# Hybrid layers and a matrix-memory block on one core: transfer order, places of the modulation chunks, and attention by pairs of heads

## What is computed

```
for l in 0, 1:                                  # two hybrid layers
    proj = x @ w_in[l]
    y = [retention(rq,rk,rv) * silu(rg),        # 4 heads of 64, rotary, decay, normalised
         nsa(nq, compressed, selected, window keys) * silu(ng),   # 8 query heads, 2 key heads
         rg_lru(conv(lx)) * silu(lg)]           # a linear recurrence over the tokens
    x = layer_norm(1.41 * x + y @ w_out[l])
# one conditioned block
sh1, sc1, g1, sh2, sc2, g2 = silu(c) @ w_ada + b_ada        # w_ada is 1024 x 6144
h_lat, h_ctx = modulate(x), modulate(ctx)       # h_ctx uses the c_ctx version of sh1, sc1
m = mlstm(h_lat, h_ctx)                         # 4 heads of 128, both directions
a = window_attention(h_lat, h_ctx, sink)        # 8 query heads, 2 key heads of 64
x = x + g1 * ((sigmoid(gm)*(m @ w_bm) + sigmoid(ga)*(a @ w_ba)) @ w_out)
x = x + g2 * peer(modulate(x))                  # 16 of 16384 experts for each token and head
```

## Time and profile before

| | |
|---|---|
| median of three executions | 1475.07 us (1467.1 to 1476.45) |
| profiled execution, device time | 1466.19 us |
| its span in the trace | 1464.3 us |
| TensorE busy | 1241.4 us (85%) |
| VectorE busy | 819.8 us (56%) |
| ScalarE busy | 283.9 us (19%) |
| GpSimd busy | 314.4 us (21%) |
| mean granted clock of TensorE | 0.927 of full |
| moved by DMA | 385.69 MB |

### The profile page before, as it was taken

How to read it: one execution, slowest core, us unless ns; L and a number is a source line. 1 busy time by engine, 2 the same in 40 slices (tenths; PEclk the granted TensorE clock), 3 DMA queues, 4 the chain that set the end, 5 groups by cost and what they waited for, 6 DMA issues and landing times.

```text
span 1464.3 us, 13967 instructions
## 1 busy us (share of the span) xinstructions
PE 1241.4 (85%) x4984; PEld 741.6 (51%) x4984; DVE 819.8 (56%) x2091; ACT 283.9 (19%) x868; POOL 314.4 (21%) x278
## 2 busy tenths in 40 slices
PE   6997799978998999998797999877877397777787
PEld 4865467845873767764356565333323143333332
DVE  0746744366522265455326667676666767767654
ACT  0113200213322112222011222111111111111111
POOL 0000000000000010000002445544444264545430
PEclk9999699988999999989798999999999699999989
DMA  7651234751222443431137899999999899999995
GB/s 302 233 230 58 115 114 160 281 224 59 115 68 105 151 149 139 172 144 58 45 128 315 296 416 420 421 421 421 420 420 420 348 421 420 421 419 422 420 421 224
DMA packets 48708, 385.69 MB, mean 263 GB/s; under 512 B 5632, under 2 KB 7424, under 8 KB 9088
## 3 DMA queue, kind: packets, MB, share of 16 engines
q0 software_dynamic: 36864, 268.45, 44.5%
q1 hardware_dynamic: 11776, 116.35, 21.1%
HBM read 383.73 MB, written 1.05 MB: 263 GB/s over the span
## 4 chain that ended last, share of the span: by engine, by line
PE 58%; DMA 27%; DVE 7%; ACT 4%; issue 2%; POOL 1%; SPq 0%; DVEq 0%; POOLq 0%; ACTq 0%
DMA arena<-peer_uv_in,arena 23%; PE bank L468 22%; PE bank L474 14%; PE bank L1003 14%; DMA wring<-w_in 2%; DMA wring<-peer_uv_in,arena 2%; PE bank L509 2%; DVE arena L1413 1%; PE bank L675 1%; DVE arena L1421 1%; DVE arena L2023 1%; PE bank L830 1%; PE bank L819 1%; ACT arena L1079 1%; PE bank L875 1%
## 5 line engine op out<-in xcount | busy, mean ns | idle before, releaser
L1003 PE MATMUL bank<-arena 128*128 128x512 f32 x480 | 231.3, 626 | 47.8 <-ACT arena L1391 24.6
L1003 PE MATMUL bank<-wring,arena 128*128 128x512 f32 x368 | 188.1, 652 | 77.8 <-ACT arena L1391 77.8
L468 PE MATMUL bank<-wring,hT 128*128 128x256 f32 (+2 forms) x672 | 211.4, 472 | 19.0 <-DMA wring<-w_in 12.6
L474 PE MATMUL bank<-hT,wring 128*128 128x256 f32 (+1 forms) x1152 | 217.7, 350 | 5.7 <-issue 2.2
L474 PEld LDWEIGHTS bank<-hT,wring 128*128 128x128 f32 x1152 | 191.5, 194 | 33.8 <-issue 10.4
L2023 DVE CUSTOM_DVE_ANT_0 arena<-arena 128x1024 f32<-128x1024 f32 x120 | 147.0, 1226 | 91.0 <-DMA arena<-peer_uv_in,arena 90.7
L1003 PEld LDWEIGHTS bank<-arena 128*128 128x128 f32 x480 | 95.0, 201 | 172.7 <-issue 141.3
L2079 POOL TENSOR_TENSOR small<-small,const 128x1 f32<-128x1 f32 (+3 forms) x18 | 16.1, 894 | 762.5 <-DVEq L1425 625.8
L468 PEld LDWEIGHTS bank<-wring,hT 128*128 128x128 f32 x672 | 129.5, 197 | 98.6 <-issue 72.4
L2103 POOL DMA_INDIRECT arena<-peer_uv_in,arena x120 | 142.3, 1186 | 142.5 <-PE bank L1003 134.7
L1003 PEld LDWEIGHTS bank<-wring,arena 128*128 128x128 f32 x368 | 71.2, 201 | 182.2 <-ACT arena L1391 106.3
(11 more groups left out here) (194 smaller groups left out, 1154.5 us busy)
## 6 DMA issues: line engine op xcount, KB each, us to landing
wring<-w_in SPq DMA_DIRECT2D x23, 2048.0 KB, 8.1
wring<-ada_in SPq DMA_DIRECT2D x12, 2048.0 KB, 8.2
wring<-wo_in SPq DMA_DIRECT2D x6, 2048.0 KB, 8.2
wring<-pq_in SPq DMA_DIRECT2D x4, 2048.0 KB, 9.0
wring<-cmp_in SPq DMA_DIRECT2D x2, 2048.0 KB, 8.8
wring<-br_in SPq DMA_DIRECT2D x2, 2048.0 KB, 10.1
wring<-w1b_in SPq DMA_DIRECT2D x2, 1120.0 KB, 8.4
const<-const_in SPq DMA_DIRECT2D x1, 2012.5 KB, 14.3
```

What stands on the lines that cost most here:

```text
L468: ins = pe.matmul(bank[:, 0:cols], lhs[k], w[:, k, 0:cols], start=(k == 0), stop=(k == n - 1))
L474: ins = pe.matmul(bank[:, at:at + n_tok], w[:, k, col:col + P], rhs[:, k, :], start=(k == 0), stop=(k == KC - 1))
L1003: ins = pe.matmul(sums_of[half][:, :], diag[:, at % NDIAG, :], v_row[slot_of[at]][:, half * 512:(half + 1) * 512], start=(n == 0), stop=(n ...
```

## The change

- **Chunk order.** Modulation chunks 0 and 1 stay in layer 0, chunks 2 and 3 go to layer 1, chunk 4 to the end of layer 1, chunks 5 to 7 into the block's projections. `w1` chunks 5 and 6 follow `cmp` directly.
- **First transfers.** x tile 0 goes first, then the identity, then the first half of `w1` chunk 1 with a semaphore of its own, its second half, x tile 1, and `w1` chunk 0 ahead of the parameters and constants. In layer 0 TensorE does `rqk` of both tiles before `lxg` of both.
- **VectorE.** `lru_scan` and `retention(0)` stand in front of the loop. No modulation in rounds 0 to 3 of either layer; chunk 4 in rounds 5 to 7 of layer 1. Chunk 5 after the last rows of `hl`, chunk 6 after the copies of `aq`, chunk 7 after the forget-gate rows.
- **Gate vectors.** `context(10..13)` leave layer 1 and stand around the projection `mq`; the first waits for `ada_bias` 2, the second for 3.
- **Attention** goes over eight rounds of two heads, one of each key group. Scores of the two use the two halves of the array's rows, values the two halves of its columns and come out transposed; probabilities are scaled before their transposes, as in the hybrid layers, so the transposes to `aT` fall away. Two branch gates stand in each of rounds 1 to 6.

The diff, cut to its core:

```diff
-            mods = [("ada", 0, n) for n in ((0, 1, 2) if layer == 0 else (3, 4, 5, 6, 7))]
+            mods = [("ada", 0, 2 * layer), ("ada", 0, 2 * layer + 1)]
             chunks += [("w1", layer, 1), ("w1", layer, 0), ("w1", layer, 2), mods[0], ("w1", layer, 3), mods[1]]
-            chunks += [("w1", layer, 4), ("cmp", layer, 0)] + mods[2:-1] + [("w1", layer, 5)]
-            chunks += [("w1", layer, 6), mods[-1]] if layer else [mods[-1], ("w1", layer, 6)]
-            if layer == DEPTH - 1:
-                chunks += [("w2c", 0, 0), ("w2c", 0, 1)]
-            chunks += [("wo", layer, 0), ("wo", layer, 1)]
-        chunks += [("w2", 0, c) for c in (4, 5, 0, 2, 1, 3)]
+            chunks += [("w1", layer, 4), ("cmp", layer, 0), ("w1", layer, 5), ("w1", layer, 6)]
+            if layer == 0:
+                chunks += [("wo", 0, 0), ("wo", 0, 1)]
+        chunks += [("w2c", 0, 0), ("w2c", 0, 1), ("wo", 1, 0), ("ada", 0, 4), ("wo", 1, 1), ("ada", 0, 5)]
+        chunks += [("w2", 0, 4), ("w2", 0, 5), ("ada", 0, 6), ("w2", 0, 0), ("w2", 0, 2), ("ada", 0, 7), ("w2", 0, 1), ("w2", 0, 3)]
...
+                x_columns(0)
+                query_rows(0)
+                if L:
+                    lru_columns(0)
+                x_columns(1)
+                query_rows(1)
+                if L == 0:
+                    lru_columns(0)
+                lru_columns(1)
...
+            def attn_scores(p):
+                t, r = rounds[p]
+                for g in range(2):
+                    half = slice(g * HD, (g + 1) * HD)
+                    bank = job(("as", 2 * p + g))
+                    finish(pe.matmul(bank[:, :], aqT[half, r, t * P:(t + 1) * P], akT[half, :], start=True, stop=True),
+                           ("as", 2 * p + g))
...
+                for s in range(4):
+                    for g in range(2):
+                        half = slice(g * HD, (g + 1) * HD)
+                        ins = pe.matmul(bank[half, r * P:(r + 1) * P], akv[:, s, P + g * HD:P + (g + 1) * HD],
+                                        softT[:, p % 2, g * 512 + s * P:g * 512 + (s + 1) * P], start=(s == 0), stop=(s == 3))
...
+            for p in range(len(rounds)):
+                attn_transposes(p)
+                if p + 2 < len(rounds):
+                    attn_scores(p + 2)
+                if p:
+                    attn_values(p - 1)
+                if 1 <= p < 7:
+                    branch_gate(2 * p - 2)
+                    branch_gate(2 * p - 1)
+            attn_values(len(rounds) - 1)
...
-                    if i == 1:
-                        for t_ in range(TT):
-                            taken(pe, ("ao", t_))
-                            transposes(("aT", t_), [a_lat[:, t_, j * P:(j + 1) * P] for j in range(4)])
...
                 nsa_scale(0)
+                lru_scan()
                 gate_rows_t(0)
                 gate_rows_t(1)
+                retention(0)
                 for p in range(len(rounds)):
...
-                    if p == 0:
-                        lru_scan()
-                    if p in (0, 1):
-                        retention(p)
-                    if p < 4:
-                        modulation(7 if L else 2, (p,))
+                    if p == 1:
+                        retention(1)
+                    if L and p >= 5:
+                        modulation(4, ((0, 1), (2,), (3,))[p - 5])
...
+            def attn_scale(p):
+                t, r = rounds[p]
+                for g in range(2):
+                    taken(dve, ("as", 2 * p + g))
+                dve.wait_ge(sem("sink_exp"), p + 1)
+                e = 2 * (p % 4)
+                link(tt(es[:, e:e + 2], es[:, e:e + 2], den[:, t, r:8:4], ALU.add))
+                link(dve.reciprocal(es[:, e:e + 2], es[:, e:e + 2]))
+                both = soft[:, p % 2, :].rearrange("p (g k) -> p g k", g=2)
+                link(tt(both, both, every(es[:, e:e + 2], 512, 2), ALU.mult), "attn_scaled")
...
+            attn_max(0)
+            attn_max(1)
+            attn_scale(0)
+            for p in range(len(rounds)):
+                bank = full(dve, ("aT_", 2 * p + 1))
+                free(dve.tensor_copy(softT[:, p % 2, 512:1024], bank[:, :]), ("aT_", 2 * p + 1))
+                if p + 1 < len(rounds):
+                    attn_scale(p + 1)
+                if p + 2 < len(rounds):
+                    attn_max(p + 2)
+                modulation(8 + p // 2, (2 * (p % 2), 2 * (p % 2) + 1))
+                if p == 4:
+                    attn_out(0)
```

More of the change, by code:

```diff
@@ L1567, in _ @@
                 free(ins, ("kcvc", L))
-                modulation(1 if L == 0 else 4)
+                modulation(2 * L + 1)
+                if L:
+                    add_bias(0, 2)
+                    gain(1, V_GMIX, "mix_gain")
                 if L == DEPTH - 1:
```

209 lines of the change are left out of this document (98 added, 111 removed).

## The result

| | before | after |
|---|---|---|
| median of the runs, us | 1474.54 (1467.1 to 1476.45, 4 runs) | 1434.99 (1433.3 to 1438.13, 4 runs) |
| profiled execution, us (span) | 1466.2 (1464.3) | 1433.3 (1431.5) |
| mean granted clock of TensorE | 0.927 | 0.93 |

The ratio is 0.9743, 95% interval 0.9705 to 0.9781: 2.6% faster, 1435 as forecast. The profiled executions stand 32.9 us apart and the medians 39.6, where the sum said 35.6: the profiled execution of the kernel before is one of its fast ones, 1466.2 where most lie near 1475. Nearly the right total hides terms that missed by up to 7 us in both directions, and most of what follows is about those.

The account below looks back on a forecast made before the run. It took TensorE, then DMA in the gathers, as successive bounds. Terms 5.0 + 13.5 + 11.3 + 6.0 - 1.9 + 0.6 + 1.1 = 35.6 us gave 1430.6 (profile) or 1439.5 (median); forecast 1435, range 1420 to 1460.

Parts of the forecast that it names:

- The frame: Whole kernel: the final gather stage is DMA-bound and untouched, so each microsecond won ahead of it comes out at the end.
- Start: First transfers: half chunk lands near 7.7 us, `rqk` starts near 8, `w1` chunk 0 is released 5.0 us earlier.
- Layer 0's loop: Modulation passes and scan leave VectorE's path, shortening TensorE's waits: 13.5 us won, bounds 10 and 16.
- the walk: Round-by-round reckoning with VectorE's durations; layer 0: round 2 at 140.4, round 3 at 147.6, round 4 at 153, round 6 at 168.
- `w1` chunk 5: Layer 1: its earlier load removes a wait of 8.27 us and 3.0 us of half clock in `rvg`: 11.3 us won.
- Layer 1's loop: Four modulation passes go and the scan moves: 6.0 us won, between 7.1 and 4.7 depending on the clock.
- Projections: End of layer 1 and the block's projections: weights queued behind modulation chunks and moved contexts cost 1.9 us, bounds +2 and -9.
- rival (2): Weight chunks queued behind VectorE's modulation each cost 8.3 + 3.0 us; with four caught the kernel ends at 1480; chance 0.05.
- Attention: Pairing heads gains 3.6 us and loses 3.0 to a low clock in the opening gap: 0.6 won, bounds -4 and +4.
- Rival (4): The clock holds through the new gaps and attention's pairs gain their 8 us: 1424 us; chance 0.12.
- Rival (3): Attention becomes bound by VectorE, exposing 2.3 us in each of six rounds, 14 us: 1449 us; chance 0.08.
- The stage behind attention: ScalarE no longer copies `aT` ahead of the exponents VectorE waits for: 1.1 us won, bounds 0 and 1.5.

Follow-up runs that it names:

- after_again: The changed kernel, unedited, run and profiled once more as the control: 1433.82 us, ratio 0.9727 to the kernel before.
- quarters: The changed kernel with the first half chunk of `w1` chunk 1 loaded as two transfers of 0.5 MB: 1434.09 us, ratio 0.9713.
- b_order: The kernel before with layer 1's `w1` chunk 5 loaded one place earlier, the eight modulation passes left where they were: 1478.95 us, ratio 1.0018.
- b_scan_in_front: The kernel before with only the scan and retention(0) moved in front of the loop, in both layers: 1466.9 us, ratio 0.9936.
- a_warm: The changed kernel with unneeded matmuls filling TensorE's waits ahead of rounds 1, 3 and 4 of layer 0's loop: 1435.01 us, ratio 0.9728.
- the gateless round: Round 2 in the changed kernel with attention's first two gates moved into the gap after the first scores: 4.5 us; whole kernel 1433.17 us.
- a_single: The changed kernel with attention head by head again, as before the change: 1448.32 us, ratio 0.9827.

## Why the prediction was right, and where its steps were not

**The frame held.** The gathers' stage kept its length (555 us of it look the same; 650.5 us from first matmul to end where there were 652.4, and 652.6 in `after_again`), so what was won ahead of them came out at the end.

**Start: right mechanism, 1 us too much.** I had the half chunk land at 7.7, at the full rate of the earlier trace rows; `rqk` started at 9.52, where the prediction asked for 8. Half the bytes took 5.8 us from issue to landing and not half of 8.8, so the rate alone does not give a landing time. With quarters `rqk` started earlier again: TensorE can begin on the first piece while the rest is under way. The Trainium skill ("DMA: Bandwidth & Descriptors", Bandwidth) has 6.15 us for a transfer of 1 MB issued from GpSimd. In this kernel 1 MB took 8.8 us, issued by SyncE with others in flight, and what the prediction drew from the page, that by it the start would win nothing, is not borne out here.

**Compression: a loss that is not the change's.** Its 256 small matmuls ran with a granted clock of 0.76 between 76 and 90 us, where it was 1.00 in the same work before, and took 1.8 us longer. No wait stands in front of them. But the compression is unchanged, `after_again` took only 0.2 us longer than before (9.1 against 8.9), and `b_order` and `b_scan_in_front`, which do not touch it, took 9.2 to 9.5 at a clock of 0.87. It varies between executions, by up to 1.8 us. Why the clock falls there stays open.

**Layer 0's loop: the step that failed is the walk.** Up to round 1 it was right to half a microsecond (131.70 and the offset of 2.2 make 133.9; I had 134.4). Round 2 was to follow at 140.4 and came at 143.7, and from there to round 4 the walk stays 3 us early. The walk used VectorE's durations and left TensorE's at full clock, and counted the wait of 2.15 us as idle time and no more; it was followed by a gate piece of 5.36, and VectorE in turn waits 3.71 us for that piece. The waits fell further than the 10 us I had named, to 6.9, and yet the loop gained only 8.4 in the first profile, 11.7 in the control: part of the waits had turned into slow matmuls. The second fault is in the costing of retention's move, which the sum let stand with its 2.8 us of idleness beside the scan's 2.7 as if the two edits had to go together. With retention left inside, the loop to round 6 is 41.4 us for 55.5 before: 14.1 us, a little more than the 13.5 that I had for the change. So the term's failure is shown as far as round 2 and for retention's place; what warm matmuls alone would have given is not, since `a_warm` overshot.

**`w1` chunk 5: right**, 11.6 for 11.3, wait and clock both as read from the earlier trace rows; and the control's is 11.6 too. `b_order` shows that the order without the passes' removal is worth nothing: there VectorE's eight passes ahead of the loop are what TensorE waits for. The prediction put the passes' removal beside the term, and it was a condition of it.

**Layer 1's loop: 0.7 below the lower of the walk's two values.** Measured 4.0, the walk gave 7.1 if the idleness does not lower the clock, 4.7 if it does. It does: the gate's piece behind that wait takes 5.36 here as well.

**Projections: right in kind, -2.8 for -1.9.** The prediction's own terms, 4 less 1.6 less 3.9, give -1.5 and not the -1.9 that it wrote. Within the stretch the block's projection was to start 4 us earlier and started 4.5 earlier, in spite of the 5.32 us that it waits for `w2` chunk 4 behind `ada` 5. Chunk 0 held TensorE for 0 to 0.9 us in the eight profiles with this order, not 1.6. What took more than forecast is the clock behind the wait: from that projection to the end of the 16.57 us piece it takes 53.2 us where the profile before has 49.4. Then come 3.4 us of contexts. But `b_order` and `b_scan_in_front`, which have the old order there and no wait for a transfer, take 52.9 us as well, so the low clock is not the wait's alone, and the -2.8 is measured against the fast one of three profiles. The prediction named a wait over 4 us as a sign against itself, and it was one: this was rival (2)'s mechanism at the price of one chunk. Undone, it gives 8.3 us against the changed kernel, 5.4 of them clock; the rival had 8.3 of wait and 3.0 of clock for a caught chunk, 11.3 in all, so its total was a third too high and its parts were the wrong way round.

Layer 1 was to end some 36 us earlier. The transposes of `hl` came 33.2 us earlier (448.91, now 415.72), and some 7 of these are contexts that moved behind it and a wait of 3.5 us that went, which the wait for `w2` chunk 4 took back; the offset at round 4 was 26.1. That sign failed with the loops' terms.

**Attention: the term that was mis-sized most, 0.6 for 7.2.** The first gate came 15.7 us behind the first scores, where 15 was forecast. The terms of the walk: head 12.1, measured 12.6; rounds 61.6, measured 59.4 (five of 10.06, the last without scores 9.0); end 4.8, measured 2.9, as TensorE puts two rounds' values together; clock 3.0, of which 1.9 are already in the head as matmuls of 1.97 and 2.08 us, and nothing comes later, since the clock was back at 536. So the walk was long at each of its three terms, by 1.4 (head without the clock), 2.2 and 1.9 us. Rival (4), the clock holds and the pairs gain 8, was the nearer one in size; its 8 has no working, as the walk with the clock held gives 3.6, and in the head the clock did not hold. Rival (3) is refuted: the gated rounds have no wait for VectorE where it had 2.3 us in each of six, and even the gateless round has only 1.37. The rule of the Trainium skill beside it ("TensorEngine Tiling (Array Packing)", PSUM Bottleneck), that emptying may become the bound, which the page says of a fourfold speed-up, does not bite here, as the gates' 7.17 us of TensorE in each round cover the copies.

**The stage behind attention: 1.1 for 0.5, and not shown.** The 1.1 us that ScalarE's copies of `aT` were to give lie inside the scatter of that stage, 181.3 to 183.0 us in three profiles of kernels that have these copies and 182.6 and 183.0 without.

**Sum.** Start, compression, the two loops, the projections and the stage behind attention missed by 11.4 us against the change, attention, chunk 5 and the gathers by 8.8 for it. That 1435 was met to the microsecond is the luck of these signs, and of a number put between the sum's 1430.6 against the profiled execution and its 1439.5 against the median.

## What to carry to other kernels

In this kernel a wait that was put on the tensor engine cost its length and then the half clock behind it, and the engine that it fed waited in turn for the slow piece; walk both engines together, at both clock levels, and compare a stretch over several profiles before a few microseconds of it are explained. In an in-order load queue, keep the weights ahead of chunks whose slot waits for a slower engine: here that order alone was worth 8 us, where the paired attention was worth 7.2 in its stretch and 13 in the median. Moving a load earlier wins only if the engine that the early work meets next is ready: in `b_order` it was VectorE, with eight passes ahead of the wanted result.

## What the hardware showed that I had not expected

One and the same program, with the same waits, ran the same 16 matmuls in 5.88 us in one execution and 3.72 in another, and the six rounds around them in 47.1 and 43.8. In attention as it was before, four profiles give two lengths: 82.09 us in the profile of before and in `a_single`, 87.57 in `b_scan_in_front` and `b_order`. The difference lies between the first scores and the end of the first gate, and everything behind is equal. In `before` and `b_order` that gate takes 3.72 us against 5.82, and the granted clock is 1.00 between 546 and 564 and 0.62 between 552 and 570:

```profile
554.64 3.72 PE L468 MATMUL bank<-wring,hT 128*128 128x256 f32 x16
```

```profile
563.98 5.82 PE L469 MATMUL bank<-wring,hT 128*128 128x256 f32 x16
```

In all seven profiles of kernels with the change's attention it was 74.9. So in these profiles the change also removes a spread, and against an execution with the longer length it wins 12.6 us there. The stretch from layer 1's round 4 to the first scores has two lengths as well, 172.1 us in `before` and 177.3 in the other two. The longer attention would fit the 13.3 us between the medians of `a_single` and the changed kernel, and both together the medians before and after standing further apart than the profiles; whether they are what separates the times near 1467 and near 1476 of the kernel before was not tried.
